# Gathering u and v rows apart, and adding the weighted v rows on VectorE

## What is computed

```
h   = rmsnorm(x, g_ffn)                          # [512, 1024]
q   = h @ w_q                                    # 8 heads x 2 halves x 128
s1, s2 = q halves . sub_keys                     # 128 scores each
v1, i1 = top_k(s1, 16);  v2, i2 = top_k(s2, 16)
sc, pos = top_k(v1[:, None] + v2[None, :], 16)   # of 256 pairs
eidx = i1 * 128 + i2 at pos                      # 16 experts per head: 128 per token
gate = softmax(sc)
act  = gelu(einsum('td,thkd->thk', h, u[eidx]))  # u, v: 16384 rows of 1024 floats
x   += einsum('thk,thkd->td', gate * act, v[eidx])
x   += sigmoid(rmsnorm(x) @ W_pg) * (p @ W_ple)
out  = rmsnorm(x)
```

## Time and profile before

| | |
|---|---|
| time, median of 3 runs | 2208.06 us (2201.22 to 2208.45) |
| span of the profiled execution, first to last instruction | 2205.8 us |
| PE busy in it | 1805.0 us (82%) |
| DVE busy | 1037.9 us (47%) |
| POOL busy | 720.3 us (33%) |
| ACT busy | 405.7 us (18%) |
| moved by DMA | 603.19 MB, 273 GB/s over the span |

### The profile page before, as it was taken

One profiled execution on the slowest core, in us unless ns is written; L12 is line 12 of the kernel. 1 busy time (PEld: TensorE's weight loads), 2 busy tenths in 40 slices (PEclk: granted clock), 3 DMA queues, 4 the chain that ended last, 5 costly groups with the idle time before them and its releaser, 6 DMA issues.

```text
span 2205.8 us, 18212 instructions
## 1 busy us (share of the span) xinstructions
PE 1805.0 (82%) x4532; PEld 840.1 (38%) x4532; DVE 1037.9 (47%) x2616; ACT 405.7 (18%) x1131; POOL 720.3 (33%) x1165
## 2 busy tenths in 40 slices
PE   7988898999897999975767787687688877778876
PEld 3464443444563445432323333233233332323332
DVE  0003544111077444486666565656556655444452
ACT  2003333100112111211121112212121222111222
POOL 0003544100013433443434434344344443434340
PEclk9975887999998999988878899898899888989997
DMA  6221000122457999988889999998999999999992
GB/s 208 76 86 39 1 0 1 38 76 76 147 195 316 383 384 375 362 357 360 351 349 360 381 350 355 369 376 355 367 367 381 356 370 376 382 379 381 388 379 88
DMA packets 92213, 603.19 MB, mean 273 GB/s; under 512 B 10300, under 2 KB 11324, under 8 KB 26349
## 3 DMA queue, kind: packets, MB, share of 16 engines
q0 software_dynamic: 73728, 536.90, 61.6%
q1 hardware_dynamic: 18412, 65.44, 8.4%
HBM read 600.16 MB, written 2.14 MB: 273 GB/s over the span
## 4 chain that ended last, share of the span: by engine, by line
PE 41%; DMA 25%; DVE 12%; issue 11%; POOL 7%; ACT 2%; POOLq 1%; SPq 1%; DVEq 0%; ACTq 0%
DMA arena<-in_uv,slot 24%; PE psum L1175 13%; PE psum L1043 5%; POOL arena L381 4%; PE psum L933 4%; PE psum L985 3%; PE psum L1013 3%; PE psum L1119 3%; PE psum L1050 2%; PE psum L1146 2%; PE psum L1091 1%; POOL slot L378 1%; DVE arena L856 1%; POOL arena L369 1%; DVE arena L779 1%
## 5 line engine op out<-in xcount | busy, mean ns | idle before, releaser
L1175 PE MATMUL psum<-arena 128*128 128x512 f32 x2048 | 1011.4, 653 | 314.5 <-ACT arena L547 314.1
L856 DVE CUSTOM_DVE_ANT_0 arena<-psum,arena 128x1024 f32<-128x1024 f32 x512 | 627.0, 1225 | 594.2 <-DMA arena<-in_uv,slot 586.8
L1175 PEld LDWEIGHTS psum<-arena 128*128 128x128 f32 x2048 | 422.3, 211 | 896.0 <-issue 499.2
L381 POOL DMA_INDIRECT arena<-in_uv,slot x512 | 509.0, 994 | 249.6 <-issue 211.0
L378 POOL COPY slot<-eidx 128x1 int32 (+1 forms) x513 | 104.0, 203 | 885.1 <-PE psum L1175 358.9
L543 ACT ACTIVATE gel<-dots 128x4 f32<-128x4 f32 x128 | 26.3, 205 | 1071.8 <-DVE dots L856 1071.8
L369 POOL TENSOR_SCALAR arena<-arena 128x256 f32<-128x256 f32 (+4 forms) x128 | 105.9, 846 | 288.6 <-DVE arena L653 215.0
L547 ACT ACTIVATE arena<-ident,wts 128x128 f32<-128x128 f32 x512 | 163.6, 390 | 48.9 <-DVE wts L860 47.2
L1043 PE MATMUL psum<-arena,ring 128*128 128x512 f32 x256 | 113.0, 600 | 0.9 <-DVE arena L675 0.9
L1013 PE MATMUL psum<-arena 128*64 128x512 f32 (+1 forms) x124 | 79.1, 750 | 18.8 <-DVE arena L668 12.3
L933 PE MATMUL psum<-arena,ring 128*128 128x512 f32 x208 | 89.8, 593 | 2.8 <-DMA ring<-in_wpack 1.5
(11 more groups left out here) (167 smaller groups left out, 1097.0 us busy)
## 6 DMA issues: line engine op xcount, KB each, us to landing
ring<-in_wpack SPq DMA_DIRECT2D x97, 512.0 KB, 4.2
arena<-in_uv,slot POOLq DMA_INDIRECT x512, 9.3
arena<-in_w_pg SPq DMA_DIRECT2D x1, 4096.0 KB, 16.8
xs<-in_x SPq DMA_DIRECT2D x4, 512.0 KB, 4.7
arena<-bias_rows SPq DMA_DIRECT2D x8, 256.0 KB, 5.7
out<-xs SPq DMA_DIRECT2D x4, 512.0 KB, 6.1
arena<-bias_rows SPq DMA_DIRECT2D x8, 128.0 KB, 3.0
arena<-in_w_ple SPq DMA_DIRECT2D x1, 1024.0 KB, 21.4
```

The lines of the kernel that those rows point to most:

```text
L381: G.indirect_dma_start(out=rows[:, b % SLOTS, :], out_offset=None, in_=a["uv"], in_offset=bass.IndirectOffsetOnAxis(ap=slot[b][:, :], axis ...
L856: V.tensor_tensor_reduce(out=junk, in0=hp2, in1=rows[:, s, 0:D], scale=1.0, scalar=0.0, op0=ALU.mult, op1=ALU.add, accum_out=dots[:, e, b: ...
L1175: last = T.matmul(ps[2 + 2 * (t % 2) + c], diag[:, s, :], rows[:, s, D + c * HALF:D + (c + 1) * HALF], start=False, stop=False)
```

## The change

- `uv` becomes two tensors `u` and `v` with rows of 4 KB. Each column is now two indirect DMAs of 0.5 MB: for each tile first 128 gathers of u rows, then 128 of v rows. There are 16 slots of 4 KB a partition in place of 8 of 8 KB, so the slots hold as many bytes as before.
- One semaphore `row_used` counts the slots that VectorE is through with; GpSimd waits on it. The copies of the index into `slot` tiles are gone: the gather reads its column of `eidx` itself.
- VectorE makes the 128 dots of a tile (`dot`), ScalarE takes gelu of all 128 at once, VectorE multiplies by the gates (`weigh`), and then VectorE adds each v row times its weight (`accumulate`), even columns into `xs`, odd ones into `odd`; `close` adds the two. The diagonals, the matmuls with them, `open_sum` and `tail_read` are gone.
- ScalarE, not VectorE, copies the next tile's normed rows to `hp2`, after the dots of a tile.
- The loops of all engines are unrolled. The queries and scores of tiles 1 to 3 run at once on TensorE and ScalarE, in place of between segments. The search for the next experts lies at dots 96 and 112 and at v rows 8 to 76; the tail of the tile before at dots 3 to 60. `tail_embed` of the last tile comes after its gate matmuls.

```diff
-SLOTS = 8
-GRP = 4
-GROUPS_T = COLS // GRP
-SEGS = (16, 8, 8, 8)
+SLOTS = 16
...
-            def refill(col, b):
-
-                pool.wait_ge(dot_ready, col - SLOTS + 2)
-                pool.wait_ge(column_used, col - SLOTS + 1 + GRP + 1)
-                pool.wait_ge(index_staged, col + 1)
-                stage(col + 1, (b + 1) % body)
-                gather(b)
...
+            for n in range(TILES * 2 * COLS):
+                t, k = divmod(n, 2 * COLS)
+                col = t * COLS + k % COLS
+                if k == 0:
+                    pool.wait_ge(experts_known, t + 2 if t else 1)
+                if n == TK:
+                    pool.wait_ge(experts_known, 2)
+                if n >= SLOTS:
+                    pool.wait_ge(row_used, n - SLOTS + 1)
+                G.indirect_dma_start(out=rows[:, n % SLOTS, :], out_offset=None, in_=a["u"] if k < COLS else a["v"],
+                                     in_offset=bass.IndirectOffsetOnAxis(ap=eidx[:, col:col + 1], axis=0)
+                                     ).then_inc(row_gathered[n % SLOTS], 16)
...
+            for k in range(KC):
+                act.wait_ge(rows_turned, KC + 2 + k + 1)
+                A.activation(h2T[:, k, P:S], ps[4 + k % 4][:, 0:S - P], ACT.Copy).then_inc(hT_ready, 1)
+            for j in range(2 * PH):
+                query_evac(j)
+            for later in range(1, TILES):
+                for c in range(4):
+                    score_evac(later, c)
             for t in range(TILES):
...
+                if t:
+                    tail_norm(t - 1)
+                    tail_gate(t - 1)
+                    tail_last_norm(t - 1)
+                act.wait_ge(row_used, 2 * COLS * t + COLS)
+                A.activation(dots[:, t % 2, :], dots[:, t % 2, :], ACT.Gelu_apprx_tanh).then_inc(gelu_ready, 1)
+                if t < TILES - 1:
+                    act.wait_ge(rows_normed, TILES + t + 2)
+                    A.activation(hp2, hn[:, t + 1, :], ACT.Copy).then_inc(dot_rows_ready, 1)
+                    gate_exp(t + 1)
...
+            def dot(t, k):
+
+                n = t * 2 * COLS + k
+                dve.wait_ge(row_gathered[n % SLOTS], 16 * (n // SLOTS + 1))
+                V.tensor_tensor_reduce(out=rows[:, n % SLOTS, :], in0=hp2, in1=rows[:, n % SLOTS, :],
+                                       scale=1.0, scalar=0.0, op0=ALU.mult, op1=ALU.add,
+                                       accum_out=dots[:, t % 2, k:k + 1]).then_inc(row_used, 1)
+
+            def weigh(t):
+                dve.wait_ge(gelu_ready, t + 1)
+                V.tensor_tensor(wts[:, t % 2, :], dots[:, t % 2, :], gate[:, t * COLS:(t + 1) * COLS],
+                                ALU.mult).then_inc(weights_ready, 1)
+                dve.wait_ge(weights_ready, t + 1)
+
+            def accumulate(t, k):
+
+                n = t * 2 * COLS + COLS + k
+                w = wts[:, t % 2, k:k + 1]
+                row = rows[:, n % SLOTS, :]
+                dve.wait_ge(row_gathered[n % SLOTS], 16 * (n // SLOTS + 1))
+                if k == 1:
+                    V.tensor_scalar(odd, row, w, None, ALU.mult).then_inc(row_used, 1)
+                    return
+                to = odd if k % 2 else xs[:, t, :]
+                if k:
+                    dve.wait_ge(row_used, n - 1)
+                V.scalar_tensor_tensor(to, row, w, to, ALU.mult, ALU.add).then_inc(row_used, 1)
+
+            def close(t):
+                dve.wait_ge(row_used, (t + 1) * 2 * COLS)
+                V.tensor_tensor(xs[:, t, :], xs[:, t, :], odd, ALU.add).then_inc(sum_out, 1)
...
             for t in range(TILES):
...
+                for k in range(COLS):
+                    dot(t, k)
+                    if t == 0 and k == 7:
                         peer_norm(1, TILES)
+                    if t:
+                        if k == 3:
+                            tail_scale(t - 1)
+                        if k == 8:
+                            tail_turned(t - 1)
+                        if k == 48:
+                            tail_add(t - 1)
+                        if k == 60:
+                            tail_out(t - 1)
                     if t < TILES - 1:
...
+                        if k == 96:
+                            top_of_halves(t + 1, 0, 8)
+                        if k == 112:
+                            top_of_halves(t + 1, 8, 16)
+                weigh(t)
+                for k in range(COLS):
+                    accumulate(t, k)
+                    if t < TILES - 1:
+                        if k == 8:
                             pair_up()
+                        if k == 16:
                             top_pairs(t + 1)
+                        if k in (28, 40, 52, 64):
+                            number_experts(t + 1, (k - 28) // 6, (k - 28) // 6 + 2)
+                        if k == 68:
                             publish(t + 1, 0, PH)
+                        if k == 76:
                             gates(t + 1)
...
+                close(t)
...
+            turn_others()
+            pe.wait_ge(hT_ready, 2 * KC + 2)
+            for j in range(2 * PH):
+                other_queries(j)
...
             for t in range(TILES):
...
+                tail_turn(t)
                 for c in range(2):
...
+                    tail_gate(t, c)
+                tail_embed(t)
...
-        "uv": np.concatenate([f["peer_u"][0], f["peer_v"][0]], axis=1),
+        "u": f["peer_u"][0],
+        "v": f["peer_v"][0],
```

226 lines of the change are left out of this document (25 added, 201 removed).

## The result

The changed kernel took 2292.11 us (median of 2289.59 to 2298.83) against 2208.06 us: a ratio of 1.041, 95% interval 1.037 to 1.045. It is 4.1% slower; forecast were 2205 us and a range of 2170 to 2262. But this is only half of the result.

| measurement | before, us | changed, us | ratio, interval |
|---|---|---|---|
| first | 2208.1 | 2292.1 | 1.041 (1.037 to 1.045) |
| after_again | 2210.3 | 2295.2 | 1.039 (1.036 to 1.042) |
| same_chip | 2206.9 | 2309.8 | 1.046 (1.042 to 1.050) |
| control_3 | 2206.4 | 2157.8 | 0.978 (0.974 to 0.981) |
| control_4 | 2206.2 | 2159.7 | 0.977 (0.974 to 0.981) |

The account below looks back on a forecast made before the run. Gathers bound the old loop; afterwards VectorE's own work and DMA were taken as nearly equal limits. First dot 679.6 + VectorE 1466 + shortfalls 20 + tail 37 = 2203 us of span, so 2205 us measured; range 2170 to 2262.

Parts of the forecast that it names:

- DMA's first shortfall: Tile 0, dots 0 to 95: VectorE there at 805, DMA's rows at 822; VectorE loses about 15 us.
- Dots: VectorE's 512 dots at 1.267 us each, read from three back-to-back dots: 649 us.
- Adds: VectorE's 512 weighted adds of v rows at 1.21 us each: 620 us.
- Rival 3: Each add waits for its whole predecessor, 1.32 us: 56 us more, 2250 us, slower; chance 0.14.
- Shortfalls of rows: VectorE short of gathered rows: about 15 us in tile 0's dots, 5 us at the end; 20 us in the sum.
- Search: Expert search on VectorE, no longer hidden in waits for gathers: 56 us, three times, 167 us.
- Rival 4: VectorE and GpSimd exclude each other fully; each add also takes a gather's 0.96 us issue: about 2695 us; chance 0.03.
- Gathers: DMA's gather of 4 KB rows, 0.524 MB: 1.33 us, half of queue 0's mean, between bounds 1.24 and 1.48.
- Rival 2: 4 KB rows are dear: 1.48 us a gather, shortfalls 112 us in place of 20, 2295 us; chance 0.13.
- Tail: From the last sum's copy-out to the span's end: 37 us against 31.9, with `tail_embed` after the gate matmuls.
- First dot: VectorE's first dot starts where it did before, at 679.65 us, as earlier VectorE work is untouched.
- rival 1: DMA keeps ahead throughout: gathers at 1.24 to 1.28 us, shortfalls almost nothing; about 2182, or 2177 us; chance 0.28.

Follow-up runs that it names:

- first: The changed kernel's first measurement, on an unrecorded chip, beside the kernel before: 2292.11 us, ratio 1.041.
- after_again: The changed kernel unaltered, measured again on another chip beside the kernel before: 2295.19 us, ratio 1.039.
- same_chip: The changed kernel unaltered, on one further chip with three variants of it: 2309.8 us, ratio 1.046.
- control_3: The changed kernel unaltered, as control for three variants on the same chip: 2157.8 us, ratio 0.978.
- control_4: The changed kernel unaltered, as control when those three variants were repeated on another chip: 2159.7 us, ratio 0.977.
- looped_dots: Changed kernel with 64 of each tile's 128 dots in loops of 16 instead of written-out code: 2158.9 us, ratio 0.979.
- pair_rows: Changed kernel where each second gather brings an 8 KB row of u and v into two slots, the others left out: 2149.8 us.
- half_rows_2: Changed kernel with each gather bringing only 2 KB of a row, VectorE's instructions kept; a repeat, 28.5 us faster than control_3.
- four edits at once: Four variants of the changed kernel, run side by side on one chip: 2161.9, 2130.1, 2159.7 and 2158.9 us.
- late search: Changed kernel with tile 1's expert search moved from tile 0's dots to its adds: 2161.9 us; on same_chip's chip 2306.3 us.
- own_wait: Changed kernel with dots writing to two fixed buffers by turns, each waiting for the dot before the last: 2159.7 us, ratio 0.979.

## Why the prediction was wrong

**The step that failed** is in the sum for DMA's first shortfall, "as TensorE now rushes through the queries", and with it that VectorE, once it has its row, goes at the pace of its rows. I took TensorE's pace under full traffic from a trace with 8 KB packets. In the first measurement it was held to a third of its pace (99 matmuls against 336 in 100 us), the scores of tile 1 came at 864 us, where control_3 has them by 782, and VectorE lost 56.3 us in one wait. In that wait the rows caught up, so tile 0 lost 45.5 us net; stalls of VectorE itself and late answers to its waits cost 24 to 29 us in each other tile. The text had named an engine that stands still as what would make it wrong, put it down to unrolled code, and gave it no price. That unrolled code is to blame no run tested, since looped_dots ran only where there were no stalls; the trace speaks against it, with three instruction packets in a stretch where TensorE alone stood 43 times. Why the engines stand stays open. The 85 us by which the forecast span of 2203 missed the first measurement are 132 us of stalls less 47 us by which it was too high without them: two errors, of which the second hid a part of the first.

**Where there are no stalls** the sum can be checked term by term, and it missed there too: 2158 us, below the range. control_3 against the prediction:

- *Dots*: 1.267 us each were forecast, 649 us. In its timeline they start 1.14 us apart (1068.11, 1069.25), and 512 x 1.144 = 586 us, 63 less. This is the term that was mis-sized most. I read the pace from three dots of the kernel before, each of which waited for its predecessor by `dot_ready`; the change took that wait away, and so the gap. The kernel before, then control_3: a dot started 0.12 us after the read of its predecessor's sum, and now starts together with it.

```profile
680.79 0.08 DVE L856 DVE_READ_ACCUMULATOR2_ANT dots<- 128x1 f32 x1
680.91 1.22 DVE L856 CUSTOM_DVE_ANT_0 arena<-psum,arena 128x1024 f32<-128x1024 f32 x1
```

```profile
1068.11 0.08 DVE L773 DVE_READ_ACCUMULATOR2_ANT dots<- 128x1 f32 x1
1068.11 1.22 DVE L773 CUSTOM_DVE_ANT_0 arena<-psum,arena 128x1024 f32<-128x1024 f32 x1
1069.25 0.08 DVE L773 DVE_READ_ACCUMULATOR2_ANT dots<- 128x1 f32 x1
1069.25 1.22 DVE L773 CUSTOM_DVE_ANT_0 arena<-psum,arena 128x1024 f32<-128x1024 f32 x1
```

  No run puts the wait back, so that it makes the gap rests on these rows and the code. The adds' pace I did read off instructions without such a wait.
- *Adds*: forecast 1.21, 620 us. Timeline, VectorE and GpSimd:

```profile
876.82 1.28 DVE L795 SCALAR_TENSOR_TENSOR arena<-arena,wts 128x1024 f32<-128x1024 f32 x1
878.02 1.28 DVE L795 SCALAR_TENSOR_TENSOR xs<-arena,wts,xs 128x1024 f32<-128x1024 f32 x1
878.02 0.94 POOL L367 DMA_INDIRECT arena<-in_v,eidx  x1 [0.30 <-issue]
879.21 1.31 DVE L795 SCALAR_TENSOR_TENSOR arena<-arena,wts 128x1024 f32<-128x1024 f32 x1
879.27 0.94 POOL L367 DMA_INDIRECT arena<-in_v,eidx  x1 [0.31 <-issue]
880.45 1.32 DVE L795 SCALAR_TENSOR_TENSOR xs<-arena,wts,xs 128x1024 f32<-128x1024 f32 x1
880.51 0.94 POOL L367 DMA_INDIRECT arena<-in_v,eidx  x1 [0.30 <-issue]
881.69 1.32 DVE L795 SCALAR_TENSOR_TENSOR arena<-arena,wts 128x1024 f32<-128x1024 f32 x1
```

  They start 1.20 us apart, the pace that was read from the kernel before, until a gather's issue begins 0.06 us behind each; then an add lasts 1.32 and the next starts 1.24 us later. In the whole trace, of adds that follow each other without a wait, the 236 with an issue begun 0.05 to 0.15 us behind their start are 1.243 us apart in the median, the 54 with none begun beside them 1.199. In pair_rows an issue begins 0.35 us behind every second add, and adds that don't wait keep 1.20:

```profile
877.09 1.28 DVE L798 SCALAR_TENSOR_TENSOR xs<-arena,wts,xs 128x1024 f32<-128x1024 f32 x1
877.44 1.74 POOL L369 DMA_INDIRECT arena<-in_uv,eidx  x1 [0.66 <-DVE arena L798]
878.28 1.28 DVE L798 SCALAR_TENSOR_TENSOR arena<-arena,wts 128x1024 f32<-128x1024 f32 x1
```

  So the gathers that the change doubles seem to cost an add 0.04 us each; no run moved the issue by itself, so this is argued. 128 adds take 156.9 us in tiles 0 to 2 and 158.9 in half_rows_2's tile 3, 630 in all, 10 more than forecast. Rival 3 (an add every 1.32 us) falls.
- *Shortfalls of rows*: 15 and 5 us forecast. Against half_rows_2 the dots of tiles 0 to 3 lose 27.8, 1.3, 0.5 and 3.8 us, and the adds' stretch of tile 3 6.2 (167.0 against 160.8). Sum 39.6, 19.6 more; since the dots are quicker, VectorE runs into the transfers' pace of 1.28 us sooner.
- *Search*: its instructions take 54.9 us a tile (56 forecast), 2.4 less in three.
- *GpSimd*: gathers' issues have a median of 0.94 us and at most 1.94. Beyond those 0.04 us an add they cost nothing. Rival 4 falls, and with it the Trainium skill's mutual lock (SBUF — State Buffer, section Who interferes with whom) for VectorE's part as I had read it: held up for a gather's whole issue an add would last 2.2 us, and it lasts 1.32.
- *Gathers*: 1.28 us, where 1.33 was taken. Rival 2 (1.48) falls as a mechanism, though its 2295 us happens to be what the first measurement gave; a time alone confirms no mechanism.
- *Tail*: 2156.0 less 2121.8 is 34.2 us, 37 forecast. The order is as forecast, the last multiplies behind `tail_embed`:

```profile
2146.07 1.28 DVE L748 TENSOR_TENSOR arena<-arena,psum 128x512 f32<-128x512 f32 x2 [20.09 <-PE psum L1086]
```

- *First dot*: 675.1 instead of 679.65 (676.8 in the first measurement). I did not follow up what brings it forward.

From the forecast span of 2203: -4.6 (first dot), -63, +10, +19.6, -2.4 (search), -2.8 (tail) and -3 for the small terms (tails of tiles 0 to 2, waits for gelu, closes) give 2156.8, and 2156.0 was measured. VectorE nearly always busy, waits for gathers in tile 0 and tile 3, DMA at 1.00 in dots (1067 to 1240) and 0.83 in the search (1250 to 1300): these signs were right. The end that was closest was rival 1 (2182, 2177): right in the gathers' pace of 1.28, and wrong in that the shortfalls would shrink; they doubled, and the time fell by the dots, which no rival had. Neither kind of measurement fell into the range of 2170 to 2262.

## What to carry to other kernels

Read an instruction's pace from rows that have the waits it will have, not only its shape: the wait that an edit removes is in the pace too (here 0.12 us in each of 512 dots, 63 us). And when an experiment "works", run the unaltered kernel beside it on the same chip; four edits at once seemed to cure a loss of 6%, which was not there without them either on such a chip (2158 us), and which one of them, the late search, did not touch where it was (2306 us).

## What the runs showed of the hardware

- Measurements on different chips differ by 6% on one program (2158 and 2290 to 2310 us) and not measurably on another (2202 to 2210 us). In the slower ones all engines stand in steps of some 0.7 us, nearly all of it in the phases of the dots, beside gathers of 4 KB rows at 400 GB/s; a matmul then comes every 1.4 to 2.8 us, and TensorE is at its pace again when the gathers pause (105 matmuls from 812 to 850). What of the kernel calls this up, and whether it needs the recording, stays open.
- Dots that read PSUM and SBUF follow each other in 1.144 us although each lasts 1.22 and is followed by 0.08 us for its accumulator; a wait for the instruction two back costs them nothing (own_wait, 2159.7 us).
- Adds of 128x1024 with two inputs in SBUF start every 1.20 us, and every 1.24 with a gather's issue begun just behind each (control_3).
- Written-out code against loops, 64 of 128 dots: no difference where there are no stalls (2158.9 and 2157.8 us).
- 8 KB rows at 422 GB/s, 4 KB rows at 409.
